# GpSimd adds the squares of two latent norms, and TensorE sums them over the channels in one product

## The chip, the cores and the metric

One Trainium2 chip, one of its cores. The metric is the device time of the whole program in microseconds (us), the median of several runs. The engines are TensorE (PE; its weight loads are PEld), VectorE (DVE), ScalarE (ACT), GpSimd (POOL) and SyncE (SP), which issues the DMAs.

## The reference, cut to what matters

Two blocks of two layers each are computed on 512 tokens; the first block also carries 256 context tokens. In the first block each layer projects the normalised input to a query latent of 384 channels and to a key/value latent of 256 channels, and both latents go through an RMS norm before they are projected on:

```
def rms_norm(x, g):
    xf = x.astype(jnp.float32)
    y = xf * lax.rsqrt(jnp.mean(xf * xf, axis=-1, keepdims=True) + EPS)
    return (y * g.astype(jnp.float32)).astype(x.dtype)

def mla_project(q_lat, kv_lat, g_qa, w_qb, g_kva, w_kvb):
    q = (rms_norm(q_lat, g_qa) @ w_qb).reshape(B, T, H_B, NOPE_B + ROPE_B)
    kv = (rms_norm(kv_lat, g_kva) @ w_kvb).reshape(B, T, H_B, NOPE_B + V_B)
```

The mean of the squares over the channels is what this case is about. Nothing else of the computation is touched.

## The kernel before, in words

Activations lie with the channels on the partitions, 128 to a tile, and the tokens along the free axis: 768 tokens in layer 0 of the first block; in its layer 1, 512 for what belongs to queries and 768 for what belongs to keys and values. The query latent (`qlb`) so has three tiles and the key/value latent (`kvlb`) two.

Every 128x128 weight product is done in three products, from a high and a low part of both operands. The weights of a unit (one output tile) come by DMA from SP into one of three RAW buffers. ScalarE copies them to a rounded high part (L1929, WH) and GpSimd subtracts to get the low part (L2627, WL). TensorE waits for the low part of a unit before its first product. The helper `ahead` sets, on ScalarE and GpSimd, the place in the queue at which these splits are done: `ahead(key)` does all units up to the one after `key`. All queues run in order.

The units of the stretch that matters are, in TensorE's order: qlb 0 to 2; qa 0 to 3 (heads' queries); kvlb 0; then the sum of squares of qlb; a rotation (`rotate_a`, L1476); kvlb 1; a rotation; krb; then the sum of squares of kvlb; a rotation; qa 4; a rotation; vch; and then the window attention. The products of qa, kvlb and krb are at L732, those of qlb at L978.

The sum of squares is `latent_sum` (L1253 on; its product is L1259). ScalarE writes the squares of each latent tile into its own SQM tile (L2114, L2149). TensorE multiplies each of them by a matrix of ones and adds them in PSUM: this sums over the channels and puts the sum on every partition. The operands are plain fp32. ScalarE then takes the root from PSUM (L1985: RSTD for the query latent, RSTDK for the other), VectorE the reciprocal (L2881), and scales the latent (L3189: GV from QLRAW). ScalarE rounds that to the high part (L1951) and GpSimd subtracts for the low part (L2635, QNL).

GpSimd's queue in `first_layer`, in order: the splits of qa 0 to 3 and kvlb 0 and 1 and krb, each set by the `ahead` one unit before; the three low parts QNL; `ahead((l, "krb", 0))`, which is the split of qa 4; `ahead((l, "qa", 4))`, which is the split of vch; later the low parts KVNL.

In layer 1 some work of layer 0's context tokens is still going on beside qa 0 to qa 3: VectorE updates XT (L2871, L2872), ScalarE squares it, VectorE adds the squares (L2852, ACC), and TensorE sums them at L940 and L945 between qa 2 and qa 3.

Of the kernel before, what the change touches and what calls it, by code (L numbers as in the profile page):

```python
# [18 lines left out]
ALU = mybir.AluOpType  # L19
# [8 lines left out]
NT = SEQ + CTX  # L28
# [145 lines left out]
class Ledger:  # L174
# [6 lines left out]
    def up(self, sem, key=None):  # L181
        n = self.count[sem.name] = self.count.get(sem.name, 0) + 1
        if key is not None:
            assert (sem.name, key) not in self.events, (sem.name, key)
            self.events[sem.name, key] = n
        return sem, 1

    def at(self, sem, key):
        if sem.name.startswith("evacuated"):
            return self.events["use", key]  # L190
        return self.known[sem.name, key] if self.known else 1
# [5 lines left out]
def program(nc, D, out, known, stop=None):  # L197
    led = Ledger(known)
    up, at = led.up, led.at
    ctx = ExitStack()  # L200
    with ctx:
# [4 lines left out]
        def place(name, shape, kb, dt=F32):  # L206
            return nc.alloc_sbuf_tensor_at(name, shape, dt, offset=BASE + int(kb * 1024))
# [26 lines left out]
        ident, ones, blockones, rot_a, rot_32, mask_prev, mask_next = (CONST[:, i * P:(i + 1) * P] for i in range(7))  # L234
# [53 lines left out]
        SQM = [place(f"SQM{i}", [P, NT], MA + 66 + 3 * i) for i in range(3)]  # L288
# [88 lines left out]
        def sem(name):  # L377
            return ctx.enter_context(nc.semaphore(name))
# [13 lines left out]
        pool_step = sem("pool_step")  # L392
# [14 lines left out]
        act_out = sem("act_out")  # L407
# [80 lines left out]
        def empty_rows(head):  # L488
            g = rope_group(head) ^ 1
            return slice(32 * g, 32 * g + 32)  # L490
# [5 lines left out]
        def segs(T):  # L496
            return [(0, SEQ)] if T == SEQ else [(0, SEQ), (SEQ, CTX)]

        def tokens(l):
            return NT if l == 0 else SEQ  # L500
# [171 lines left out]
        def _(pe):  # L672
# [4 lines left out]
            def open_group(key, g=None):  # L677

                if g is None:
                    if group[0] % 4 == held[0]:  # L680
                        group[0] += 1
                    g = group[0] % 4
                    group[0] += 1
                led.events["slot", key] = g
                if uses[g]:
                    pe.wait_ge(evacuated[g], uses[g])
                if other_half[g]:
                    sem, read = other_half[g]
                    pe.wait_ge(sem, at(sem, read))
                    other_half[g] = None  # L690
                uses[g] += 1
                led.events["use", key] = uses[g]
                return psum[g] if g < 4 else None
# [383 lines left out]
            def sum_tokens(tb, ps):  # L1077
                pe.wait_ge(to_pe, at(to_pe, ((0, "pre"), "sq", tb)))
                for k in range(KD):
                    ins = nc.tensor.matmul(ps[:, tb * P:(tb + 1) * P], ones, XIN[:, tb, k * P:(k + 1) * P],  # L1080
                                           start=k == 0, stop=k == KD - 1)
                return ins
# [31 lines left out]
            total = open_group((0, "pre"))  # L1114
# [6 lines left out]
            for tb in range(NTB - 2, NTB):  # L1121
                ins = sum_tokens(tb, total)
# [129 lines left out]

            def latent_sum(l, name, n, T):  # L1253

                ps = open_group((l, name))
                for i in range(n):
                    pe.wait_ge(act_out, at(act_out, ((l, name), "sq", i)))
                    for t0, tn in segs(T):
                        ins = nc.tensor.matmul(ps[:, t0:t0 + tn], ones, SQM[i][:, t0:t0 + tn], start=i == 0,  # L1259
                                               stop=i == n - 1)  # L1260
                ins.then_inc(*up(product_ready, (l, name)))

            def qr_load(l, t):
# [542 lines left out]
            for tb in range(NXB):  # L1806
                ps = open_group(("outT", tb))
                for k in range(KD):
                    ins = nc.tensor.transpose(ps[:, k * P:(k + 1) * P], XT[:, k, tb * P:(tb + 1) * P], ident)
# [807 lines left out]
        def _(pool):  # L2617
# [14 lines left out]
            def low(key, L, H, T):  # L2632
                n = at_split(key)
                pool.wait_ge(split_high, at(split_high, key))
                nc.gpsimd.tensor_tensor(L, GV[n % 2][:, 0:T], H.bitcast(F32), ALU.subtract).then_inc(  # L2635
                    *up(split_low, key))
# [20 lines left out]
            def gates(l, b, T):  # L2657
                for m0 in range(0, KD, 2):
                    ahead((l, "wb", b, m0))
                    ahead((l, f"g{b}", m0))  # L2660
                    ahead((l, f"g{b}", m0 + 1), 2 if b == 2 else 1)
                    if b == 2:
                        for m in (m0, m0 + 1):
                            low((l, "m", m), ML[:, m, 0:T], MH[:, m, 0:T], T)

            def first_layer(l):
                T = tokens(l)
                ahead((l, "qlb", 2), 0)
                for j in range(4):
                    ahead((l, "qa", j))  # L2670
                for j in range(2):
                    ahead((l, "kvlb", j))
                for j in range(3):
                    low((l, "qn", j), QNL[:, j, 0:T], QNH[:, j, 0:T], T)
                ahead((l, "krb", 0))
                ahead((l, "qa", 4))
                ahead((l, "vch", 0))
                for j in range(2):
                    low((l, "kvn", j), KVNL[:, j, :], KVNH[:, j, :], NT)
                for t in range(2):  # L2680
                    ahead((l, "wqr", t))
                last = len(window_units(l)) - 1
                pool.wait_ge(product_ready, at(product_ready, ("A", l, last, "o")))
                for t in range(2):
                    pool.wait_ge(w_low, led.count[w_low.name])
                    for head in range(4 * t, 4 * t + 4):
                        nc.gpsimd.memset(QS[empty_rows(head), head, 0:T], 0.0).then_inc(
                            *up(pool_out, (l, "empty", t) if head % 4 == 3 else None))
                        pool.wait_ge(pool_out, led.count[pool_out.name])
                    ahead((l, "wq", t))  # L2690
                ahead((l, "wk"))
                ahead((l, "wv"))
                for b in (1, 0):
                    if b:
                        ahead((l, Z1[b], 0))
                        pool.wait_ge(to_pe, at(to_pe, ("B", l, "inv")))
                    widened(l, b, 0, T)
                    ahead((l, Z1[b], 0))
                    widened(l, b, 1, T)
                    for j in range(4):  # L2700
                        ahead((l, Z1[b], j), 2 if j < 3 else 1)
                        low((l, "y", b, j), YLE[:, j, 0:T], YHE[:, j, 0:T], T)
                        if j < 2:
                            widened(l, b, j + 2, T)
                    gates(l, b, T)
                for j in range(4):
                    for name in ("cc", "uc", "bc", "zc"):
                        ahead((l, name, j), 2 if name == "zc" else 1)
                    low((l, "y", 2, j), YL[:, j, 0:T], YH[:, j, 0:T], T)
                gates(l, 2, T)  # L2710
                for m in range(KD):
                    ahead((l, "wo", m), 1 if l or m < KD - 1 else 0)
                if l == 0:
                    ahead((1, "qlb", 0), 0)
                    key = (1, "pre")
                    for i in range(1, KD - 1):
                        pool.wait_ge(act_out, at(act_out, (key, "sq", i)))
                        if i == 1:
                            led.events[pool_step.name, (key, "add", 0)] = led.count[pool_step.name] + 1
                        nc.gpsimd.tensor_tensor(ACC[:, 0:SEQ], SQ[0][:, 0:SEQ] if i == 1 else ACC[:, 0:SEQ],  # L2720
                                                SQ[i % 2][:, 0:SEQ], ALU.add).then_inc(*up(pool_step, (key, "add", i)))
                        pool.wait_ge(pool_step, led.count[pool_step.name])
                else:
                    norm = ("2", 0, "n", 0)
                    entry = [key for key, _, _ in entry_units(norm)]
                    ahead(entry[2], 0)
                    add_halves(norm, 0)
                    ahead(entry[3], 0)
                    ahead(entry[4], 0)
                    add_halves(norm, 1)  # L2730
# [967 lines left out]
```

## Time and profile before

| | us |
|---|---|
| median of 3 runs | 3040.29 (3038.69 to 3043.32) |
| the profiled execution, its own time | 3050.49 |
| its span, first to last instruction | 3048.7 |

| engine | busy us | share |
|---|---|---|
| PE | 2974.1 | 98% |
| PEld | 2439.6 | 80% |
| DVE | 1552.4 | 51% |
| ACT | 1197.6 | 39% |
| POOL | 1098.7 | 36% |

Times in the rows are us from the start of the span unless they say ns. In a timeline row stand the start, the duration, the engine, the line, the operation, what it writes from what, and how many instructions are merged in the row; in brackets stands how long the engine was idle before it and what released it. An fp32 product takes several passes, and each appears as more than one record. Ends of matmuls are modelled, so the start of one to the start of the next is the safer duration.

### The profile page before, as it was taken

How to read it: one execution, taken by the hardware profiler on the slowest of the kernel's cores; microseconds unless marked ns; L12 is line 12 of the kernel's file. 1: busy time of each engine (PE TensorE's matmuls, PEld its weight loads, DVE VectorE, ACT ScalarE, POOL GpSimd, SP SyncE). 2: the span in 40 equal slices, each digit the busy share in tenths (PEclk: the TensorE clock that was granted, in tenths of full speed). 3: DMA queues.
4: the chain of work that ended last, by engine and by line, in shares of the span. 5: the costliest groups of instructions: out<-in, count | busy, mean ns of one | idle time of the engine just before them, and what ended most of it. 6: DMA issues, size and time to landing. Idle time of an engine off the chain costs nothing.

```text
span 3048.7 us, 44661 instructions
## 1 busy us (share of the span) xinstructions
PE 2974.1 (98%) x17911; PEld 2439.6 (80%) x17911; DVE 1552.4 (51%) x2051; ACT 1197.6 (39%) x2017; POOL 1098.7 (36%) x561
## 2 busy tenths in 40 slices
PE   8999999999999999999999999999999999999999
PEld 6877688888888877788888877788878877788887
DVE  4364546563223586622323876477753876454420
ACT  3255431212223455423234445544332545544422
POOL 1302032423344222055456321345554321345543
PEclk9999999999999999999999999999999999999999
DMA  7102024342222233344434212146665312123332
GB/s 231 37 8 42 1 71 138 90 132 69 64 63 67 58 96 91 91 116 106 112 96 120 62 45 62 36 133 185 187 186 167 85 46 62 48 84 97 97 97 90
DMA packets 442377, 279.73 MB, mean 92 GB/s; under 512 B 113610, under 2 KB 419516, under 8 KB 441788
## 3 DMA queue, kind: packets, MB, share of 16 engines
q1 hardware_dynamic: 442172, 276.87, 32.6%
q8 instruction: 144, 2.36, 0.3%
q14 instruction: 61, 0.50, 0.0%
HBM read 274.73 MB, written 2.10 MB: 91 GB/s over the span
## 4 chain that ended last, share of the span: by engine, by line
PE 55%; DVE 3%; POOL 2%; ACT 1%; issue 1%; DMA 1%; ACTq 0%; DVEq 0%; SPq 0%; POOLq 0%
PE ps L732 33%; PE ps L1543 4%; PE ps L1052 2%; PE ps L1604 2%; PE ps L1611 2%; PE ps L1633 2%; PE ps L991 1%; PE ps L1323 1%; POOL WL L2627 1%; PE ps L1678 1%; PE ps L902 1%; PE ps L1353 1%; PE ps L1334 1%; PE ps L1709 1%; PE ps L1578 1%
## 5 line engine op out<-in xcount | busy, mean ns | idle before, releaser
L2627 POOL TENSOR_TENSOR WL<-RAW,WH 128x1024 fp32r<-128x1024 f32 (+2 forms) x335 | 804.7, 2402 | 1516.7 <-ACT WH L1929 1490.8
L732 PE MATMUL ps<-HH,WH 128*128 128x512 f32 (+1 forms) x2080 | 690.0, 369 | 6.0 <-POOL WL L2627 4.9
L732 PE MATMUL ps<-HH,WL 128*128 128x512 f32 (+1 forms) x2080 | 686.0, 367 | 0.0
L732 PE MATMUL ps<-HL,WH 128*128 128x512 f32 (+1 forms) x2080 | 682.7, 366 | 0.0
L1929 ACT ACTIVATE WH<-RAW 128x1024 fp32r<-128x1024 f32 (+2 forms) x335 | 346.4, 1034 | 408.2 <-PE ps L732 255.8
L732 PEld LDWEIGHTS ps<-HH,WH 128*128 128x128 f32 x2080 | 358.7, 188 | 81.1 <-POOL WL L2627 12.2
L732 PEld LDWEIGHTS ps<-HH,WL 128*128 128x128 f32 x2080 | 357.1, 188 | 64.9
L732 PEld LDWEIGHTS ps<-HL,WH 128*128 128x128 f32 x2080 | 356.8, 188 | 65.0
L2967 DVE SCALAR_TENSOR_TENSOR XT<-RAW,CS,XT 128x1024 f32<-128x1024 f32 x77 | 134.7, 1750 | 37.0 <-DMA RAW<-in_w_ada 36.1
L732 PE MATMUL ps<-FH,WH 128*128 128x512 f32 x308 | 120.6, 392 | 0.9 <-POOL WL L2627 0.8
L732 PE MATMUL ps<-FH,WL 128*128 128x512 f32 x308 | 120.0, 390 | 0.0
L732 PE MATMUL ps<-FL,WH 128*128 128x512 f32 x308 | 120.0, 390 | 0.0
L2967 DVE SCALAR_TENSOR_TENSOR MSUM<-RAW,CS,MSUM 128x1024 f32<-128x1024 f32 x63 | 107.0, 1735 | 12.8 <-DMA RAW<-in_w_mod 11.3
L1323 PE MATMUL ps<-KS,QS 128*128 128x512 f32 (+1 forms) x252 | 86.8, 480 | 5.8 <-ACT GV L2024 2.8
L1543 PE MATMUL ps<-HH,WH 128*128 128x512 f32 x208 | 88.6, 426 | 3.5 <-POOL WL L2627 3.0
L2635 POOL TENSOR_TENSOR FL<-GV,FH 128x512 fp32r<-128x512 f32 x44 | 57.5, 1307 | 90.6 <-ACT FH L1951 90.6
L3058 DVE TENSOR_REDUCE NMAX<-ps 128x1 f32<-128x768 f32 (+1 forms) x80 | 66.0, 847 | 41.7 <-PE ps L1323 40.4
L2586 ACT ACTIVATE UB<-ps,VEC 128x512 f32<-128x512 f32 x44 | 34.3, 780 | 132.6 <-PE ps L732 132.6
L3644 DVE SCALAR_TENSOR_TENSOR XT<-ps,MOD,XT 128x512 f32<-128x512 f32 x14 | 10.5, 751 | 142.9 <-PE ps L732 142.9
L1543 PE MATMUL ps<-HH,WL 128*128 128x512 f32 x208 | 81.5, 392 | 0.0
L1543 PE MATMUL ps<-HL,WH 128*128 128x512 f32 x208 | 81.2, 390 | 0.0
L1951 ACT ACTIVATE FH<-GV 128x512 fp32r<-128x512 f32 x44 | 27.8, 632 | 135.7 <-DVE GV L3631 135.7
(557 smaller groups left out, 5722.6 us busy)
## 6 DMA issues: line engine op xcount, KB each, us to landing
RAW<-in_w_in SPq DMA_DIRECT2D x122, 512.0 KB, 3.9
RAW<-in_w_ada SPq DMA_DIRECT2D x96, 512.0 KB, 3.9
RAW<-in_w_up SPq DMA_DIRECT2D x88, 512.0 KB, 4.3
RAW<-in_w_in SPq DMA_DIRECT2D x72, 256.0 KB, 3.7
RAW<-in_w_mod SPq DMA_DIRECT2D x32, 512.0 KB, 3.7
RAW<-in_w_down SPq DMA_DIRECT2D x32, 512.0 KB, 4.7
WMOD<-in_w_mod SPq DMA_DIRECT2D x8, 1024.0 KB, 14.2
RAW<-in_w_branch SPq DMA_DIRECT2D x16, 512.0 KB, 3.4
```

Source lines behind the costliest of these rows:

```text
L732: ins = nc.tensor.matmul(ps[0:width, t0:t0 + tn], a, b[:, k0 + k, tokens0 + t0:tokens0 + t0 + tn], start=first and k == 0 and i == 0, stop ...
L1052: ins = nc.tensor.matmul(groups[n][:, half(p)], a, b[:, k, half(p)], start=k == 0 and t == 0, stop=k == KD - 1 and t == 2)
L1323: ins = nc.tensor.matmul(half[:, c:c + m], QS[:, 2 * j + h, qs], KS[2 * j + h][:, start:start + m], start=True, stop=True)
L1543: ins = nc.tensor.matmul(ps[:, 0:SEQ], lhs, rhs[:, k, 0:SEQ], start=k == 0 and i == 0, stop=k == KD - 1 and i == 2)
L1604: nc.tensor.matmul(ps[:, 512 * h:512 * h + 512], QN2[a][hs, j, qb * P:(qb + 1) * P], QN2[a][hs, 3, :], start=True, stop=True).then_inc(*up ...
L1611: ins = nc.tensor.transpose(ps[:, b * P:(b + 1) * P], P2[n % 2][h][:, b * P:(b + 1) * P], ident)
L1633: ins = nc.tensor.matmul(o[hs, qb * P:(qb + 1) * P], VN2[a][:, b, hs], PT2[n % 2][h][:, b * P:(b + 1) * P], start=b == 0, stop=b == NXB - 1)
L1929: A(weight_tiles(units[n][3])[0][:, 0:used], RAW[n % NRAW][:, 0:used], ACT.Copy).then_inc(*up(w_high))
L2627: nc.gpsimd.tensor_tensor(wl[:, 0:used], RAW[n % NRAW][:, 0:used], wh[:, 0:used].bitcast(F32), ALU.subtract).then_inc(*up(w_low))
L2635: nc.gpsimd.tensor_tensor(L, GV[n % 2][:, 0:T], H.bitcast(F32), ALU.subtract).then_inc(*up(split_low, key))
L2967: V.scalar_tensor_tensor(total, row, c, total, ALU.mult, ALU.add).then_inc(*done)
L3058: V.tensor_reduce(NMAX[:, 2 * n + h:2 * n + h + 1], ps[:, 0:keys], AX.X, ALU.max, negate=True).then_inc(*up(to_act, ("B", l, n, h)))
```

## The change

`latent_sum` on TensorE does one product for each span of tokens, over SQM[0] alone, in place of one for each tile, and waits for GpSimd's last add before it. GpSimd gets a new function, `add_squares`, which adds SQM[1] and, for the query latent, SQM[2] into SQM[0]; it waits for ScalarE's squares before each add and for its own add after it. For the query latent it stands behind the split of qa 2, for the key/value latent behind the split of qa 4 and ahead of the split of vch. Both layers of the first block have it.

```diff
             def latent_sum(l, name, n, T):
 
+                pe.wait_ge(pool_step, at(pool_step, (l, name, "add", n - 1)))
                 ps = open_group((l, name))
-                for i in range(n):
-                    pe.wait_ge(act_out, at(act_out, ((l, name), "sq", i)))
-                    for t0, tn in segs(T):
-                        ins = nc.tensor.matmul(ps[:, t0:t0 + tn], ones, SQM[i][:, t0:t0 + tn], start=i == 0,
-                                               stop=i == n - 1)
+                for t0, tn in segs(T):
+                    ins = nc.tensor.matmul(ps[:, t0:t0 + tn], ones, SQM[0][:, t0:t0 + tn], start=True, stop=True)
                 ins.then_inc(*up(product_ready, (l, name)))
...
+            def add_squares(l, name, n, T):
+
+                for i in range(1, n):
+                    for part in (i - 1, i):
+                        pool.wait_ge(act_out, at(act_out, ((l, name), "sq", part)))
+                    total = SQM[0][:, 0:T]
+                    nc.gpsimd.tensor_tensor(total, total, SQM[i][:, 0:T], ALU.add).then_inc(
+                        *up(pool_step, (l, name, "add", i)))
+                    pool.wait_ge(pool_step, led.count[pool_step.name])
+
             def first_layer(l):
                 T = tokens(l)
                 ahead((l, "qlb", 2), 0)
                 for j in range(4):
                     ahead((l, "qa", j))
+                    if j == 1:
+                        add_squares(l, "qlb", 3, T)
                 for j in range(2):
                     ahead((l, "kvlb", j))
                 for j in range(3):
                     low((l, "qn", j), QNL[:, j, 0:T], QNH[:, j, 0:T], T)
                 ahead((l, "krb", 0))
+                add_squares(l, "kvlb", 2, NT)
                 ahead((l, "qa", 4))
```

## Rows read from the trace of the kernel before

**Rows 1.** The page: busy time of the engines, and the chain that ended last.
```profile
PE 2974.1 (98%) x17911; PEld 2439.6 (80%) x17911; DVE 1552.4 (51%) x2051; ACT 1197.6 (39%) x2017; POOL 1098.7 (36%) x561
PE 55%; DVE 3%; POOL 2%; ACT 1%; issue 1%; DMA 1%; ACTq 0%; DVEq 0%; SPq 0%; POOLq 0%
```
**Rows 2.** Timeline of TensorE, layer 0, around both sums.
```profile
118.76 4.03 PE L1259 MATMUL ps<-SQM,CONST 128*128 128x512 f32 x12
122.63 1.02 PE L1476 MATMUL ps<-QA,CONST 128*128 128x512 f32 x2
...
141.15 2.74 PE L1259 MATMUL ps<-SQM,CONST 128*128 128x512 f32 x8
143.73 1.02 PE L1476 MATMUL ps<-QA,CONST 128*128 128x512 f32 x2
145.08 0.62 PE L732 MATMUL ps<-HH,WH 128*128 128x512 f32 x2 [0.33 <-POOL WL L2627]
```
**Rows 3.** The same of layer 1.
```profile
1053.89 2.74 PE L1259 MATMUL ps<-SQM,CONST 128*128 128x512 f32 x6
1056.47 1.02 PE L1476 MATMUL ps<-QA,CONST 128*128 128x512 f32 x2
...
1074.99 2.74 PE L1259 MATMUL ps<-SQM,CONST 128*128 128x512 f32 x8
1077.57 1.02 PE L1476 MATMUL ps<-QA,CONST 128*128 128x512 f32 x2
1078.03 0.92 PE L732 MATMUL ps<-HH,WH 128*128 128x512 f32 x2
```
**Rows 4.** Timeline of GpSimd, layer 0.
```profile
95.36 2.39 POOL L2627 TENSOR_TENSOR WL<-RAW,WH 128x1024 fp32r<-128x1024 f32 x1 [6.09 <-ACT WH L1929]
...
142.23 2.80 POOL L2627 TENSOR_TENSOR WL<-RAW,WH 128x1024 fp32r<-128x1024 f32 x1
147.38 2.43 POOL L2627 TENSOR_TENSOR WL<-RAW,WH 128x1024 fp32r<-128x1024 f32 x1 [2.35 <-ACT WH L1929]
```
**Rows 5.** The same of layer 1.
```profile
1026.28 2.40 POOL L2627 TENSOR_TENSOR WL<-RAW,WH 128x1024 fp32r<-128x1024 f32 x1 [6.67 <-ACT WH L1929]
1031.95 2.39 POOL L2627 TENSOR_TENSOR WL<-RAW,WH 128x1024 fp32r<-128x1024 f32 x1 [3.28 <-ACT WH L1929]
...
1073.40 2.83 POOL L2627 TENSOR_TENSOR WL<-RAW,WH 128x1024 fp32r<-128x1024 f32 x1
```
**Rows 6.** GpSimd's two-input operations by line (ns min/median/max).
```profile
L2720 POOL TENSOR_TENSOR ACC<-ACC,SQ x5: 1267/1295/1312, 981.2 to 987.8; 128x512 f32<-128x512 f32 x5
L2635 POOL TENSOR_TENSOR YLE<-GV,YHE x8: 1830/1851/2196, 409.2 to 581.1; 128x768 fp32r<-128x768 f32 x8
```
**Rows 7.** Timeline of ScalarE, layer 0, from the query latent's root on.
```profile
119.79 1.28 ACT L1985 ACT_TABLE_LOAD   x1
122.83 0.90 ACT L1985 ACTIVATE RSTD<-ps,epsb 128x768 f32<-128x768 f32 x1 [1.76 <-PE ps L1259]
...
132.17 0.81 ACT L2145 ACTIVATE KVRAW<-ps 128x768 f32<-128x768 f32 x1 [6.76 <-PE ps L732]
133.01 0.85 ACT L2149 ACTIVATE SQM<-KVRAW 128x768 f32<-128x768 f32 x1
133.76 1.56 ACT L1951 ACTIVATE QNH<-GV 128x768 fp32r<-128x768 f32 x2
```
**Rows 8.** Timeline of VectorE, layer 1, beside GpSimd's splits.
```profile
1027.81 1.14 DVE L2852 TENSOR_TENSOR ACC<-SQ,SQ 128x256 f32<-128x256 f32 x1
...
1029.97 0.43 DVE L2852 TENSOR_TENSOR ACC<-ACC,SQ 128x256 f32<-128x256 f32 x1
...
1031.41 0.43 DVE L2852 TENSOR_TENSOR ACC<-ACC,SQ 128x256 f32<-128x256 f32 x1
...
1074.02 2.76 DVE L3007 TENSOR_TENSOR QA<-QA,T1a 128x512 f32<-128x512 f32 x1
```
**Rows 9.** Timeline of TensorE, layer 1, where it waits for VectorE's adds.
```profile
1036.21 0.58 PE L940 MATMUL ps<-CONST,ACC 128*128 128x1 f32 x4 [0.48 <-DVE ACC L2852]
```
**Rows 10.** Stretches (us, busy of PE and its records, granted clock) and the waits around them.
```profile
1945.97 0.47 PE L732 MATMUL ps<-MIXH,WH 128*128 128x512 f32 x1 [2.86 <-issue]
...
1943.00:1945.90 2.90, 0.11 (x2) 1.00 0.00 0
1947.40:1950.70 3.30, 3.30 (x9) 0.50 0.00 0
```

## The prediction

> **What bounds the kernel now.** I read the page's engine list and the chain of waits first: TensorE is busy 98% of the span, and no other engine over 51% [rows 1]. So a product taken from TensorE is worth its time, if nothing else makes TensorE wait there. Then I read TensorE's timeline at the four sums, to see what each costs and what it waits for next; the reader is to see that the second sum of layer 0 is followed by a wait of 0.33 us for a low part from GpSimd [rows 2]. Then the queue of GpSimd at those places, since the new adds stand in it [rows 4, 5], ScalarE's for what shifts [rows 7], and VectorE's, which suffers beside GpSimd [rows 8].
>
> **What TensorE sheds.** From first product to the following rotation the query sum takes 122.63 - 118.76 = 3.87 us in layer 0 for three tiles, 1.29 each; two go: 2.58 us. The key/value sum takes 143.73 - 141.15 = 2.58 us for two, one goes: 1.29 us [rows 2]. In layer 1 the query sum, on 512 tokens, takes 2.58 us, 0.86 each; two go: 1.72 us. The key/value sum sheds 1.29 us again [rows 3]. Together 6.88 us, 0.23% of the time. That is the most it can bring.
>
> **What GpSimd gets.** An fp32 add of 512 columns takes 1.29 us there, a two-input operation of 768 columns 1.83 us undisturbed [rows 6]. Layer 0: two adds of 1.83 us, then one; layer 1: two of 1.29 us, then one of 1.83 us.
>
> **Query adds, layer 0: hidden.** They stand before the split at 95.36, ahead of which GpSimd is idle 6.09 us [rows 4]; two adds take 3.7 us, the squares are long there, and TensorE asks for them only at 118.76. Cost nothing; the 2.58 us are gained at that point. Without the idle time it would still be covered by the 20 us up to TensorE's sum.
>
> **Query adds, layer 1: hidden from the sum, not from VectorE.** GpSimd is idle 3.28 us between the splits at 1026.28 and 1031.95 [rows 5], the adds take 2.6 us. But VectorE's add of 256 columns takes 0.43 us alone and 1.14 us where a split of GpSimd is under way; it ended 0.3 us after the split. L3007 likewise took 2.76 us beside the split at 1073.40 and ended behind it [rows 5, 8]. An operation of VectorE with two inputs in SBUF waits for GpSimd's to end, and the reverse. Now adds fall on the VectorE adds at 1029.97 and 1031.41. Worked through: first add 1028.95 to 1030.25, VectorE's until 1030.7; second add until 1032.0, VectorE's until 1032.4 in place of 1031.84; the next split and the VectorE add behind it shift alike. TensorE already waits 0.48 us for the last of those adds [rows 9], so 0.6 us come onto its path. Bounds: 0 if the adds fall between, 1.3 us if both VectorE adds wait for a whole add; I take 0.6, the worked order. The Trainium skill says this outright (SBUF — State Buffer, section "SBUF: two separate sides"): the port pair that both engines share is an exclusive lock for the whole instruction, and an operation of VectorE with two SBUF inputs takes it; the trace agrees (1.14 against 0.43 us).
>
> **Key/value add, layer 0: on the path.** GpSimd's split of qa 4 ends at 145.03, and TensorE begins qa 4 at 145.08 [rows 2, 4]. The add is queued behind that split, and TensorE's sum, which stands ahead of qa 4, waits for the add. What is upstream moves forward by 2.58 us: ScalarE's KVRAW copy waits for TensorE (6.76 us idle before it), the QNH behind it and the low parts follow; the root of the query latent gains only 1.7 us, since the table load ends at 121.07, but its successors have the slack [rows 7]. So krb's products end at 138.57, the split of qa 4 at 142.45. VectorE's waiting small operation goes first (0.1), the add takes 1.83 us, the signal 0.05: 144.43. The remaining sum takes 1.29 us and the rotation 0.46 (1077.57 to 1078.03 [rows 3]): qa 4 begins at 146.18 in place of 145.08. TensorE stands idle 5.9 us and all that was shed is gone: **+1.1 us**. Behind the wait on TensorE are the sum, rotation, qa 4 and vch; on ScalarE, which waits for this sum, the Exp table and the split of vch: about 3 to 4 us later than the 147.38 of [rows 4], needed only 8.5 us after qa 4 begins, so no cost.
>
> **Key/value add, layer 1: on the path.** The same order: krb's products end at 1074.99 - 1.72 = 1073.27, the split at 1076.23 - 1.72 = 1074.51, then L3007 takes its 0.7 us first (it did so behind the same split [rows 8]) until 1075.06, the add until 1076.89, signal, sum and rotation 1.80: qa 4 begins at 1078.69 in place of 1078.03. TensorE idle 3.7 us: **+0.66 us**. With the 0.6 above, +1.26 us.
>
> **The clock.** Where TensorE stood nearly idle for 2.9 us (busy 0.11), its granted clock was 1.00 up to the restart and soon after 0.50, that is 1.2 in place of 2.4 GHz, from about 1947.3 to 1950.7 [rows 10]. Products there go at half pace, so 3.4 us yield 1.8 us of work: 1.6 us lost. The two new idle stretches (5.9 and 3.7 us) are longer than that one, so I take one such loss for each: **+3.2 us**. Bounds: 0 (if the fall comes and goes while TensorE is idle) and 4.8 us (half as much again for each). The Trainium skill warns of the same (TensorE: Matmul & The Clock Gate, "HAM oscillation — how this bites in real kernels"): gaps in TensorE's work throw its clock back to half, and the next work begins cold. By it this change should lose twice; the trace agrees for a gap of 2.9 us.
>
> **Sum.** 1.1 + 1.26 + 3.2 = 5.6 us more. On the profiled execution 3050.49 gives 3056.1. That one lies 10.2 us over the median of the runs, and nothing in the sum scales with it, so on the median: 3040.29 + 5.6 = 3045.9, 0.18% more.
>
> **Rivals.** (a) The clock does not fall, or in one stretch only: +2.4 to +4.0 us, 3042.7 to 3044.3. For it: a wait of 0.33 or 0.48 us brings none, so there is a point below which nothing happens; against it, 2.9 us was enough. (b) Slower: the clock stays at half longer after a longer idle stretch, since the restart comes at another point: 3.2 us more of loss for the two, +8.8 us, 3049.1. For it: the 5.9 us have no like in the trace, and the sum itself and the rotation would then run at half pace; against it: the one stretch seen was of 3.4 us. It decides as soon as 0.5 us are added to my sum, since that passes +0.2%. (c) The change brings what it sheds: the kv add is ready when TensorE gets there, as it would be if krb's split chain had slack: -6.88 us, 3033.4. Against it is the order of GpSimd's queue, with qa 4's split ending 3.9 us after krb's products already; for it, nothing but the size of the saving. (d) Only the wait of layer 0 is real, since layer 1's split of qa 4 starts earlier than I shift it: 1.1 + 1.6 there, 0.6 - 1.72 - 1.29 in layer 1, +0.3 us, 3040.6.
>
> **How the numbers follow.** Forecast 0.44; (a) 0.20; (b) 0.27; (c) 0.04; (d) 0.05. A measurement of this kernel tells 0.2%, 6.1 us, from no change. The forecast lies 0.5 us below that, so a quarter of its chance counts as slower: 0.27 + 0.11 = 0.38. Faster 0.04, same 0.58. The range reaches from (d), 3040.5, which takes in the clock's lower bound, to beyond (b), 3050, and leaves out (c) and half of what lies beside (b).
>
> **What would show it.** The profile after should have 14 records at L1259 in place of 34; TensorE idle some 6 and 3.7 us before two of the sums, released by GpSimd's add, and no idle before the query sums; a granted clock of 0.5 behind each of the two; one longer VectorE add near 1030. The forecast is wrong if the adds end before krb's products, or if TensorE's idle time is short in both places.

## The result, and the profile after

The changed kernel takes 3053.36 us (median of 6 runs, 3051.81 to 3056.13) against 3045.03 us before (6 runs, the three from above among them): ratio 1.0028, 95% interval 1.0018 to 1.0037. By the medians that is 8.3 us more, where 5.6 were forecast and called no change. Measured again later beside other kernels, it was 1.0023 (1.0015 to 1.0032), 7 us. The change makes the kernel slower: both intervals lie above 1. A ratio is not the quotient of the two medians, so the two can differ by 1 or 2 us; below, a gain or a loss of whole runs in us is from the ratio unless the medians are named.

The page of the profile after: engines' busy time, which answers to [rows 1].
```profile
PE 2968.1 (97%) x17891; PEld 2435.6 (80%) x17891; DVE 1562.2 (51%) x2051; ACT 1197.3 (39%) x2017; POOL 1108.3 (36%) x567
```
TensorE has 20 instructions fewer and its busy time fell by 6.0 us, which includes work at half clock; GpSimd has the six adds more.

Timeline of TensorE after the change, at the query sum and the key/value sum of layer 0, which answers to [rows 2]; last the rotation behind qa 4.
```profile
118.27 1.45 PE L1258 MATMUL ps<-SQM,CONST 128*128 128x512 f32 x4
119.56 1.02 PE L1474 MATMUL ps<-QA,CONST 128*128 128x512 f32 x2
...
143.75 2.93 PE L1258 MATMUL ps<-SQM,CONST 128*128 128x512 f32 x4 [5.51 <-POOL SQM L2670]
146.48 1.91 PE L1474 MATMUL ps<-QA,CONST 128*128 128x512 f32 x2
147.40 1.63 PE L732 MATMUL ps<-HH,WH 128*128 128x512 f32 x2
...
156.90 1.02 PE L1474 MATMUL ps<-QA,CONST 128*128 128x512 f32 x2
```
The query sum takes 1.29 us to the next rotation, as worked out. At the key/value sum TensorE stands idle for 5.51 us, and GpSimd's add ends it. The same one-product sum then takes 2.73 us to its rotation in place of 1.29, and the rotation 0.92 in place of 0.46: half pace.

The same of layer 1, the key/value sum, which answers to [rows 3].
```profile
1074.90 2.92 PE L1258 MATMUL ps<-SQM,CONST 128*128 128x512 f32 x4 [3.31 <-POOL SQM L2670]
1077.62 1.91 PE L1474 MATMUL ps<-QA,CONST 128*128 128x512 f32 x2
1078.55 1.63 PE L732 MATMUL ps<-HH,WH 128*128 128x512 f32 x2
...
1088.37 1.02 PE L1474 MATMUL ps<-QA,CONST 128*128 128x512 f32 x2
```
GpSimd's timeline after the change around the adds (layer 0, then layer 1), which answers to [rows 4, 5].
```profile
88.74 3.74 POOL L2670 TENSOR_TENSOR SQM<-SQM,SQM 128x768 f32<-128x768 f32 x2
...
139.15 2.79 POOL L2625 TENSOR_TENSOR WL<-RAW,WH 128x1024 fp32r<-128x1024 f32 x1
141.91 1.79 POOL L2670 TENSOR_TENSOR SQM<-SQM,SQM 128x768 f32<-128x768 f32 x1
...
1028.52 2.92 POOL L2670 TENSOR_TENSOR SQM<-SQM,SQM 128x512 f32<-128x512 f32 x2
...
1069.82 2.82 POOL L2625 TENSOR_TENSOR WL<-RAW,WH 128x1024 fp32r<-128x1024 f32 x1
1072.60 2.25 POOL L2670 TENSOR_TENSOR SQM<-SQM,SQM 128x768 f32<-128x768 f32 x1
```
Stretches of TensorE after the change (us, busy and records, granted clock): the idle time of layer 0 in two parts and the work behind it, then the same of layer 1. They answer to [rows 10].
```profile
138.10:141.40 3.30, 0.14 (x2) 1.00 0.00 0
141.60:143.60 2.00, 0.00 (x0) 0.65 0.17 27
143.80:148.30 4.50, 4.50 (x7) 0.50 0.17 27
1073.40:1074.80 1.40, 0.00 (x0) 0.73 0.69 176
1074.90:1080.10 5.20, 5.20 (x9) 0.50 0.11 45
```
A granted clock of 1.00 is 2.4 GHz and 0.50 is 1.2 GHz. The clock falls while TensorE is still idle and stays at half for the sum, the rotation and the first products of qa 4.

**A local yardstick.** Whole executions of one kernel differ by 10 us and more here (reasons stand at the end), so I also compare the stretch in which the change lies: from the start of the query sum to the rotation behind qa 4. Two rows of before are needed for its ends.
```profile
153.67 1.02 PE L1476 MATMUL ps<-QA,CONST 128*128 128x512 f32 x2
1086.76 1.02 PE L1476 MATMUL ps<-QA,CONST 128*128 128x512 f32 x2
```
With the starts in [rows 2, 3] that is 34.91 us in layer 0 (153.67 - 118.76) and 32.87 in layer 1. For all kernels, one execution each, from the same starts in their timelines:

```
kernel                         layer 0  layer 1   against before
before                          34.91    32.87
changed                         38.63    36.17    +3.72 +3.30 = +7.0
changed, second execution       39.12    36.28    +4.21 +3.41 = +7.6
query latent only               32.32    30.99    -2.59 -1.88 = -4.5
key/value latent only           41.39    36.84    +6.48 +3.97 = +10.5
changed, TensorE kept busy      36.09    33.29    +1.18 +0.42 = +1.6
add behind the second low part  34.63    30.44    -0.28 -2.43 = -2.7
split of qa 4 first             32.42    31.59    -2.49 -1.28 = -3.8
split and rotation first        30.44    29.86    -4.47 -3.01 = -7.5
that order, sums as before      34.15    32.86    -0.76 -0.01 = -0.8
```
This yardstick has an error of its own: from one rotation to the next the same products take 9.34 us before (122.63 to 131.97) and 9.17 in the kernel with the key/value latent only (121.36 to 130.53), both at full clock. A stretch has three such intervals, so differences of up to about 0.5 us in it say nothing.

### The profile page after: what moved, and what is told of

It is laid out like the page before. It is cut to its first block, busy times and chain, and to the rows that moved or that the text cites. A ratio compares the mean times of both kernels' runs of the same rounds, so it can differ in the third digit from the quotient of the medians.

```text
span 3049.9 us, 44633 instructions
## 1 busy us (share of the span) xinstructions
PE 2968.1 (97%) x17891; PEld 2435.6 (80%) x17891; DVE 1562.2 (51%) x2051; ACT 1197.3 (39%) x2017; POOL 1108.3 (36%) x567
## 4 chain that ended last, share of the span: by engine, by line
PE 55%; DVE 3%; POOL 1%; ACT 1%; issue 1%; DMA 0%; ACTq 0%; DVEq 0%; POOLq 0%
PE ps L732 33%; PE ps L1541 4%; PE ps L1052 2%; PE ps L1609 2%; PE ps L1602 2%; PE ps L1631 2%; PE ps L991 1%; PE ps L1321 1%; PE ps L1676 1%; POOL WL L2625 1%; PE ps L902 1%; PE ps L1351 1%; PE ps L1332 1%; PE ps L1707 1%; PE ps L1576 1%
## 5 line engine op out<-in xcount | busy, mean ns | idle before, releaser
L3655 DVE SCALAR_TENSOR_TENSOR XT<-ps,MOD,XT 128x512 f32<-128x512 f32 x14 | 10.5, 751 | 142.1 <-PE ps L732 142.1
```

## The experiments

### Each half alone

The theory: all that is lost is lost at the key/value sums, where TensorE waits for an add queued behind the split of qa 4 and its clock falls; the query half is gained. The rival: GpSimd's adds disturb VectorE or a queue, so that the query half costs too. The first kernel leaves out the key/value half:

```diff
-                latent_sum(l, "kvlb", 2, NT)
+                latent_sum_each(l, "kvlb", 2, NT)
...
-                add_squares(l, "kvlb", 2, NT)
```
`latent_sum_each` is the sum of before.

> The change for the query latent alone; the key/value latent is summed by TensorE as before. My theory (the whole loss is at the key/value sums, where TensorE waits for GpSimd's add and its clock falls): the query adds are hidden, TensorE sheds 2.58 + 1.72 us, so about 4.3 us less than before, ratio 0.9986, and no new stretch at half clock. Rival (the adds on GpSimd hold up VectorE beside qa 2 in layer 1, or shift the chain elsewhere): 0 or more, ratio 1.0 or above.

Measured: 3040.84 us against 3045.03, ratio 0.9980 (0.9971 to 0.9989), 6 us less by the ratio and 4.2 by the medians; local stretch -4.5 us. The query half gains what was shed, and TensorE waits at neither of its sums. The second kernel has the other half alone (`latent_sum_each` for qlb, without `add_squares` for it).

> The change for the key/value latent alone; the query latent is summed by TensorE as before. My theory: the split of qa 4 ends where it did, and add, signal, sum and rotation come behind it: +3.7 us in layer 0 and +2.4 us in layer 1; the clock falls twice as in the changed kernel, +5.7 us: together +11.8 us, ratio 1.0039. Rival (only the waits cost, the clock's fall is paid by nothing): +6.1 us, 1.0020. Rival (the query adds are the cause): near 1.0.

Measured: 3051.53, ratio 1.0023 (1.0015 to 1.0032), 7 us; local stretch +10.5 us. It is slower, as the theory has it, and the query adds are cleared. The size is less than the 11.8 us expected, and by the whole runs alone the rival in which only the waits cost (1.0020) fits better; against it stand the local stretch and the next experiment. In layer 1 the clock was at half for a shorter time, since it fell only after the sum had begun; what else the difference between local stretch and whole run comes from I did not settle. The timeline of TensorE in this kernel, layer 1, and the clock before and behind the fall:
```profile
1079.03 2.18 PE L1268 MATMUL ps<-SQM,CONST 128*128 128x512 f32 x4 [3.33 <-POOL SQM L2680]
1081.01 1.91 PE L1484 MATMUL ps<-QA,CONST 128*128 128x512 f32 x2
1081.93 1.55 PE L732 MATMUL ps<-HH,WH 128*128 128x512 f32 x2
1083.31 0.51 PE L732 MATMUL ps<-HL,WH 128*128 128x512 f32 x2
...
1079.10:1079.80 0.70, 0.70 (x2) 1.00 0.75 304
1079.90:1083.20 3.30, 3.30 (x7) 0.50 0.00 1
```
The second product of qa 4 is already at full pace, where in the changed kernel it is the fourth. The wait is as long as there, 3.33 against 3.31 us, but the clock is at half for about 3.4 us in place of 6.8: the length of the wait alone does not set the price.

### The wait without the clock

TensorE gets products of a constant to do while it waits; nobody uses what they give.

```diff
                 ps = open_group((l, name))
+                if name == "kvlb":
+                    for _ in range((8, 12)[l == 0]):
+                        nc.tensor.matmul(ps[:, 768:1024], ones, CONST[:, 0:256], start=True, stop=True)
+                pe.wait_ge(pool_step, at(pool_step, (l, name, "add", n - 1)))
```

> The whole change, but TensorE works while it waits for GpSimd's add: 12 (layer 0) and 8 (layer 1) products of the ones matrix with 256 constant columns into an unused part of the sum's own PSUM group, some 0.43 us each, ahead of the wait. If the clock is what costs: no fall to half there, 5.7 us come back, about +1.3 us over before, ratio 1.0004. If the wait alone costs: as the changed kernel, +7 to +8 us, 1.0025. Should the clock cost only what I forecast (3.2 us): +4 us, 1.0013.

Measured: 3048.22, ratio 1.0007 (0.9998 to 1.0016), 2 us; local stretch +1.6 us. TensorE in this kernel: filler, a rest of the wait, the sum at full pace, and the clock of the stretches of filler and of sum.
```profile
138.15 5.34 PE L1258 MATMUL ps<-CONST 128*128 128x256 f32 x24
143.84 1.56 PE L1261 MATMUL ps<-SQM,CONST 128*128 128x512 f32 x4 [0.36 <-POOL SQM L2673]
145.24 1.02 PE L1477 MATMUL ps<-QA,CONST 128*128 128x512 f32 x2
...
138.20:143.40 5.20, 5.20 (x25) 1.00 0.04 6
143.80:148.30 4.50, 4.46 (x19) 1.00 0.18 29
```
The sum starts at the same time as in the changed kernel (143.84 against 143.75), so the wait is the same; only the clock differs. Locally 7.0 - 1.6 = 5.4 us come back, about three quarters of the loss. In whole runs it is 1.0023 - 1.0007 of the time, 5 us, by the second measurement of the changed kernel, and 1.0028 - 1.0007, 6 us, by the first.

### The add at another place in GpSimd's queue

```diff
                 for j in range(3):
                     low((l, "qn", j), QNL[:, j, 0:T], QNH[:, j, 0:T], T)
+                    if j == 1:
+                        add_squares(l, "kvlb", 2, NT)
                 ahead((l, "krb", 0))
-                add_squares(l, "kvlb", 2, NT)
```

> The whole change, but GpSimd does the key/value add behind the second low part of the query latent, where it is idle, and no longer behind the split of qa 4. Position theory: TensorE does not wait at the sum; it waits at qa 4 for the split, 3.1 us in layer 0 and 0.6 us in layer 1, and qa 4 begins 1.7 and 2.6 us earlier than before the change: -4.3 us, 0.9986, or -2 us with one fall of the clock behind the 3.1 us. Rival (GpSimd's adds cost as such, wherever they stand): slower than before, 1.001 or more.

Measured: 3045.02 against 3046.93, ratio 0.9992 (0.9983 to 1.0001), 2 us less, which the interval does not tell from no change; local stretch -2.7 us. The same add, earlier in GpSimd's queue (at 134.60 in place of 141.91 in layer 0), and the kernel is not slower: the place costs, not the add. TensorE now waits in layer 0 for the split of qa 4, for less long, and the clock falls even so:
```profile
142.19 0.62 PE L732 MATMUL ps<-HH,WH 128*128 128x512 f32 x2 [2.41 <-POOL WL L2625]
...
142.80:146.00 3.20, 3.20 (x13) 0.54 0.41 65
```

### The add and the split ahead of the query latent's parts

What the add is queued behind is the split of qa 4, and that stands behind the query latent's high and low parts, which nobody needs ahead of the window attention. On GpSimd:

```diff
-                for j in range(3):
-                    low((l, "qn", j), QNL[:, j, 0:T], QNH[:, j, 0:T], T)
                 ahead((l, "krb", 0))
                 add_squares(l, "kvlb", 2, NT)
+                for j in range(3):
+                    low((l, "qn", j), QNL[:, j, 0:T], QNH[:, j, 0:T], T)
```
and on ScalarE `ahead((l, "krb", 0))` likewise ahead of the three `high((l, "qn", j), ...)`.

> The whole change, and on ScalarE and GpSimd the split of qa 4 and then the key/value add stand ahead of the query latent's high and low parts, which are needed only behind the window attention. My theory: the add is ready before krb's products end, TensorE waits at neither sum, and all that was shed is gained: -6.9 us, ratio 0.9977, no stretch at half clock there. Rival (VectorE's rotation, now late behind the query latent's parts, holds the PSUM group that qa 4 wants, or the late query parts are needed): 0 to -3 us.

Measured: 3042.33 against 3045.03, ratio 0.9995 (0.9985 to 1.0006), not told from no change; local stretch -3.8 us. The rival holds: no wait at the sum, but another in its place, 1.75 us in layer 0 and 1.50 in layer 1. The waits of TensorE in this kernel between 120 and 170 us (total, times, longest):
```profile
PE ps L732 <- DVE QA L3016: 1.7, 1, 1.7
PE ps L1391 <- DVE KA L3018: 0.3, 1, 0.3
```
qa 4 waits for the PSUM group that VectorE's rotation of head tile 1 frees, and that rotation stands behind the last query part, now late. So VectorE does it one step earlier:

```diff
                     ins.then_inc(*valued((l, "qn", j)))
+                    if j == 1:
+                        rotate_a(l, 1)
                 dve.wait_ge(split_value, led.count[split_value.name])
-                rotate_a(l, 1)
```

> As the kernel with the split of qa 4 first, and VectorE also does the rotation of head tile 1 ahead of the last query part, so that the PSUM group that qa 4 takes is free in time (qa 4 waited 1.7 and 1.5 us for it). My theory (what the change sheds is real once nothing waits): no wait of TensorE at either place, -6.9 us, ratio 0.9977. Rival (another wait takes its place, the first scores of the window attention waiting for VectorE): -3 to -4 us, 0.9989.

Measured: 3039.59 against 3046.93, ratio 0.9978 (0.9969 to 0.9986), 6.7 us less by the ratio and 7.3 by the medians; local stretch -7.5 us. The timeline of TensorE in this kernel, layer 0:
```profile
138.88 0.51 PE L732 MATMUL ps<-HH,WL 128*128 128x512 f32 x2
139.23 1.45 PE L1258 MATMUL ps<-SQM,CONST 128*128 128x512 f32 x4
140.52 1.02 PE L1474 MATMUL ps<-QA,CONST 128*128 128x512 f32 x2
140.98 0.91 PE L732 MATMUL ps<-HH,WH 128*128 128x512 f32 x2
```
krb's last product, the sum, the rotation and qa 4 follow one another without a gap. Is that the order's merit or the sum's? The same order with the sums of before:

> The order of that kernel on ScalarE, GpSimd and VectorE, but the sums as before the change: TensorE does all five products for each layer and GpSimd adds nothing. It leaves the change out. My theory: the order by itself is worth the 0.33 us that qa 4 waited in layer 0, ratio 0.9999, and the difference to the last kernel is what the products cost, 6.6 us. Rival (the order is the gain): as the last kernel.

Measured: 3046.51, ratio 0.9997 (0.9988 to 1.0005); local stretch -0.8 us. The order alone is worth next to nothing: it takes away the wait of 0.33 us ahead of qa 4 in layer 0, and in layer 1 it changes nothing. Between this kernel and the last lie 6.7 us locally and 6.9 us by the medians (3046.51 - 3039.59): the change is worth the 6.88 us of the sum once nothing waits, and this version beats both kernels: by 0.22% the one before, by 0.45% the changed one measured beside it.

### The changed kernel again

The two halves measured apart would give 1.0003 together (0.9980 and 1.0023), the whole had been 1.0028 at another time. So it ran once more, beside three of the kernels above.

> The changed kernel itself, beside the next three. From the trace: waits +1.2 us net of what was shed, two falls of the clock that cost 2.7 and 3.0 us: about +7 us, ratio 1.0023. The sum of the two halves measured before (0.9980 and 1.0023) would be 1.0003; if that holds instead, the first comparison of the change owed several us to something that no part of it does.

Measured: 3053.48 against 3046.93, ratio 1.0023 (1.0015 to 1.0032), 6.6 us by the medians. Both whole measurements (8.3 and 6.6) and the two local stretches (7.0 and 7.6) lie at 7 to 8 us. The half with the key/value latent alone is the one that measured low against its own trace: +10.5 us locally, where its interval ends at 9.7. Locally the halves give 10.5 - 4.5 = 6.0, 1 us under the whole, and the shorter time at half clock in layer 1 of that half, 3.4 us less of it, is large enough to account for it. The stretches of this execution show the clock once more: at half from before the sum on, in both layers.
```profile
143.20:148.40 5.20, 5.20 (x9) 0.50 0.15 23
1074.90:1080.20 5.30, 5.30 (x9) 0.50 0.12 49
```

## Why the prediction was wrong

The order of things was right; the step that failed is the price of the clock, put at 3.2 us where the runs show 5.4, and with it the side of the 0.2% on which the time came out.

- **What TensorE sheds: right.** 2.59 and 1.88 us locally for the query half alone, against 2.58 and 1.72; with the order mended the whole gives -7.5 us locally and 6.7 in runs, against 6.88; against the same order with the sums of before it is -6.7 and 6.9.
- **Query adds, layer 0: right.** 3.74 us at 88.74, done long before the next split at 94.92.
- **Query adds, layer 1, on VectorE: wrong, 0.6 us too much.** VectorE's adds, which I had worked out to be held up, took no longer than before, and TensorE waits 0.54 us for the last of them in place of the 0.48 of [rows 9]:
```profile
1029.86 0.42 DVE L2863 TENSOR_TENSOR ACC<-ACC,SQ 128x256 f32<-128x256 f32 x1
...
1031.30 0.42 DVE L2863 TENSOR_TENSOR ACC<-ACC,SQ 128x256 f32<-128x256 f32 x1
```
  GpSimd's two adds took 2.92 us together in place of 2.6 (1028.52 to 1030.00 and 1030.08 to 1031.44). Each of the two VectorE adds began 0.14 us before one of them ended and was not held, which is the case I had put as the lower bound; I had the first begin 0.28 us before the end and wait. VectorE is still held where it meets more of a GpSimd operation: its next add, which fell on a split, took 1.84 us, as it had before (1.78). The Trainium skill (SBUF — State Buffer, "SBUF: two separate sides") says that the one who starts first has the port pair for the whole instruction; that agrees with the 1.84 us, and an overlap of 0.14 us in the records cost nothing. Such a term can't be had closer than its bounds.
- **Key/value add, the waits: right.** Idle 5.51 and 3.31 us against 5.9 and 3.7. What the waits and the sheds come to without the clock was 1.1 + 0.66 us in my sum; the kernel with TensorE kept busy shows 1.18 + 0.42, the same within the yardstick's error.
- **The clock: right mechanism, the size wrong, and it decided.** I took 1.6 us for each fall, from the one stretch of 3.3 us at half clock behind an idle time of 2.9 us [rows 10]. The two falls cost 38.63 - 36.09 = 2.5 us and 36.17 - 33.29 = 2.9 us, 5.4 in place of 3.2. The stretch at half clock was longer: the clock fell about 1.5 and 0.9 us before the restart (that is what 0.65 and 0.73 of the idle stretches mean) and full pace came back only near 149 and 1081, some 6.8 us after the fall, where [rows 10] show half as much. Of that, 5.3 and 6.0 us lay over work, and about half of that is what the falls cost. My bound of 4.8 us for both was too low. This is rival (b), to which I gave 0.27: a longer time at half clock behind the restart. Its condition, a longer idle stretch, is not borne out: the kernel with the key/value latent only has 3.4 us at half clock behind a wait of 3.33 us, the changed one 6.8 us at a wait of 3.31. Why it is one or the other stays open. Its own figure, 6.4 us for the clock, was somewhat too high, and its total of +8.8 us stands beside 8.3 and 6.6 measured.
- **What rival (a) rested on: misread.** I wrote that a wait of 0.48 us brings no fall. In the profiled execution of before the clock did fall soon behind that wait, which stands among products of one column:
```profile
1035.70:1037.90 2.20, 1.41 (x12) 1.00 1.27 177
1039.40:1042.70 3.30, 3.30 (x11) 0.50 0.00 0
```
  In that of the changed kernel there was none at the same place, at a wait of 0.54 us. So the price of the clock was read from one fall although the same trace had others, and a single execution does not tell whether a short wait brings one.
- **The sum.** 1.2 + 0.4 + 0 + 5.4 = 7.0 us, 0.23%; I had 1.1 + 0.66 + 0.6 + 3.2 = 5.6, 0.18%. Since the forecast lay 0.5 us from the boundary, its best value should have carried a chance of slower near one half; I counted a quarter of it. The range was placed on a median of 3040.29 that itself moved to 3045.03 with more runs, so the measured 3053.36 lies outside of it although the difference, 8.3 us, is within the range's 9.7. A range on an absolute time needs the spread of before in it, 3038.69 to 3043.32 with three runs.

The Trainium skill's rule that I had named (TensorE: Matmul & The Clock Gate, "HAM oscillation — how this bites in real kernels"), that gaps bring the clock down and the work behind them runs cold, was borne out twice in each of the two profiled executions of the changed kernel, and even by a gap of 2.41 us; a gap of 2.86 us elsewhere in the changed kernel brought no fall (last section).

## What to carry to other kernels

When work is moved from the bounding engine to an idle one, read the queue of the idle one at that place, not its share of busy time: two adds of 1.8 and 2.3 us cost 7 us because each stood behind a split that was itself just in time. Price a new gap on TensorE as the gap plus the clock's fall behind it; here the falls cost 5.4 us where the waits, less what was shed, cost 1.6, and filling the gaps with products that nobody needs gave the 5.4 back. Then look whether something in that queue is needed later than it stands: with two reorderings that are worth nothing by themselves the same change gained 0.22%.

## What the runs showed of the hardware

- All six waits of TensorE of 3.3 us or more at these sums (5.51 and 3.31 us in two executions of the changed kernel, 5.51 and 3.33 with the key/value latent only) brought the granted clock from 2.4 to 1.2 GHz, and so did one of 2.41 us. Waits of 1.75 and 1.50 us, in the kernel with the split of qa 4 first, did not. Between them it is not the length alone: the wait of 2.86 us of [rows 10], at which the clock fell before the change, left it at full in the profiled execution of the changed kernel:
```profile
1948.88 0.47 PE L732 MATMUL ps<-MIXH,WH 128*128 128x512 f32 x1 [2.86 <-issue]
...
1948.90:1954.00 5.10, 5.10 (x23) 1.00 0.01 3
```
- How long the clock stays at half differs in the same way. Behind a wait of 1.06 us near 989, in code that the change doesn't touch, it was about 3.4 us before the change, 6.8 in the changed kernel, and none with the key/value latent only:
```profile
991.70:994.90 3.20, 3.20 (x17) 0.50 0.76 161
988.80:995.40 6.60, 6.60 (x32) 0.50 0.38 79
990.50:1000.00 9.50, 9.50 (x81) 1.00 0.37 78
```
- The same code runs at one of two paces at full clock. Three products of a 768-token tile took 1.06 us in the profiled execution of before and 1.04 us in that of the changed kernel, at a granted clock of 1.00 in both. Timelines of TensorE, before and then changed:
```profile
799.73 0.51 PE L732 MATMUL ps<-HH,WH 128*128 128x512 f32 x2
...
800.79 0.51 PE L732 MATMUL ps<-HH,WH 128*128 128x512 f32 x2
```
```profile
800.45 0.51 PE L732 MATMUL ps<-HH,WH 128*128 128x512 f32 x2
...
801.49 0.39 PE L732 MATMUL ps<-HH,WH 128*128 128x512 f32 x1
```
  This is most of why the two profiled executions differ by 1.3 us only (3050.49 and 3051.81) while their local stretches differ by 7: from a split that begins at 531.58 before and 535.20 in the changed kernel to one at 976.20 and 974.51, with the clock at full in both, the changed one makes up 5.3 us, of which 0.9 are shorter waits of TensorE. What sets the pace I did not find; it changes within an execution. Together with falls of the clock that come and go elsewhere it makes single executions of this kernel differ by more than 0.2%.
